# Head norms of a differential attention two at a time, and five waits moved, in an encoder trunk on one core

## The reference

```python
s = einsum('bhcqd,bhckd->bhcqk', q_blk, kt) * scale + bias      # two maps (c) for each of 4 heads
p = softmax(s, axis=-1)
a = p[:, :, 0] - lam * p[:, :, 1]
o = einsum('bhqk,bhkv->bhqv', a, vt)                            # 128 channels a head
o = rms_norm(o, subln_g) * (1.0 - lam_init)                     # per head, over its 128 channels
mixed = concatenate([u, o.reshape(B, T, DIFF_WIDTH)], axis=-1)  # u: the convolution module, 512 channels
h = h + mixed @ w_out
```

## Time and profile before

| | |
|---|---|
| time, median of 3 runs | 1874.54 us (1874.12 to 1876.93) |
| profiled execution | 1874.37 us |
| its span, first to last instruction | 1872.6 us |
| mean granted TensorE clock | 0.995 |
| PE busy | 1821.2 us (97%) |
| DVE busy | 1310.9 us (70%) |
| ACT busy | 829.0 us (44%) |
| POOL busy | 160.0 us (9%) |

### The profile page before, as it was taken

The page is one execution under the profiler, slowest core; times in us unless marked ns, Lnnn a source line. Parts: engine busy times, 40 slices in busy tenths (PEclk is TensorE's granted clock), DMA queues, the critical chain, the costliest instruction groups (busy, mean ns, idle before and its releaser), DMA issues.

```text
span 1872.6 us, 38843 instructions
## 1 busy us (share of the span) xinstructions
PE 1821.2 (97%) x16913; PEld 1495.9 (80%) x16913; DVE 1310.9 (70%) x1716; ACT 829.0 (44%) x1085; POOL 160.0 (9%) x127
## 2 busy tenths in 40 slices
PE   6999999999999999999999999999999999999998
PEld 4898657778888888885779999898778788888886
DVE  5898665435878687857748888887574347787867
ACT  4434675335544434423644334343553346343445
POOL 1000002001000000110002222222110010000001
PEclk9999999999999999999999999999999999999999
DMA  6226323203152331453432122112442113405231
GB/s 219 69 90 212 109 80 134 90 23 103 55 179 63 118 123 57 144 174 124 162 141 72 51 52 56 52 32 71 150 159 90 46 45 113 153 27 180 65 116 57
DMA packets 149842, 189.95 MB, mean 101 GB/s; under 512 B 11881, under 2 KB 119958, under 8 KB 148010
## 3 DMA queue, kind: packets, MB, share of 16 engines
q1 hardware_dynamic: 146352, 174.97, 29.3%
q0 software_dynamic: 3088, 12.45, 1.7%
q10 hardware_dynamic: 234, 0.06, 0.0%
HBM read 161.75 MB, written 21.51 MB: 98 GB/s over the span
## 4 chain that ended last, share of the span: by engine, by line
PE 52%; DVE 3%; ACT 1%; issue 1%; DMA 1%; DVEq 0%; ACTq 0%; SPq 0%
PE ps L408 10%; PE ps L410 10%; PE ps L409 10%; PE ps L2645 7%; PE ps L2611 2%; PE ps L2658 2%; PE ps L2599 1%; PE ps L1979 1%; PE ps L2019 1%; PE ps L2622 1%; PE ps L1397 1%; PE ps L2741 1%; PE ps L2578 1%; PE ps L2670 1%; PE ps L1378 1%
## 5 line engine op out<-in xcount | busy, mean ns | idle before, releaser
L372 DVE TENSOR_TENSOR weights_split<-w,weights_split 128x2048 fp32r<-128x2048 f32 x117 | 267.9, 2290 | 116.4 <-ACT weights_split L354 102.9
L354 ACT ACTIVATE weights_split<-w 128x2048 fp32r<-128x2048 f32 x118 | 226.3, 1918 | 266.8 <-PE ps L410 249.1
L408 PE MATMUL ps<-x_hn_hi,weights_split 128*128 128x512 f32 x640 | 252.4, 394 | 0.0
L410 PE MATMUL ps<-x_hn_hi,weights_split 128*128 128x512 f32 x640 | 249.2, 389 | 0.0
L409 PE MATMUL ps<-x_hn_lo,weights_split 128*128 128x512 f32 x640 | 249.0, 389 | 0.0
L408 PE MATMUL ps<-weights_split,f_hidden_hi 128*128 128x512 f32 x448 | 175.5, 392 | 0.0
L410 PE MATMUL ps<-weights_split,f_hidden_lo 128*128 128x512 f32 x448 | 174.5, 389 | 0.0
L409 PE MATMUL ps<-weights_split,f_hidden_hi 128*128 128x512 f32 x448 | 174.5, 389 | 0.0
L408 PEld LDWEIGHTS ps<-x_hn_hi,weights_split 128*128 128x128 f32 x640 | 120.2, 188 | 25.6 <-issue 1.0
L409 PEld LDWEIGHTS ps<-x_hn_lo,weights_split 128*128 128x128 f32 x640 | 120.2, 188 | 25.6 <-issue 1.0
L410 PEld LDWEIGHTS ps<-x_hn_hi,weights_split 128*128 128x128 f32 x640 | 120.1, 188 | 25.2
(11 more groups left out here) (395 smaller groups left out, 3771.8 us busy)
## 6 DMA issues: line engine op xcount, KB each, us to landing
w<-in_ffn_w_up_dram SPq DMA_DIRECT2D x24, 1024.0 KB, 7.4
w<-in_ffn_w_down_dram SPq DMA_DIRECT2D x24, 1024.0 KB, 5.3
w<-in_xattn_w_kv_dram SPq DMA_DIRECT2D x15, 1024.0 KB, 5.5
w<-in_ab_w_in_dram SPq DMA_DIRECT2D x10, 1024.0 KB, 5.1
w<-in_xattn_w_q_dram SPq DMA_DIRECT2D x8, 1024.0 KB, 5.2
w<-in_xattn_w_o_dram SPq DMA_DIRECT2D x8, 1024.0 KB, 5.1
f_weights<-in_ffn_w_up_dram SPq DMA_DIRECT2D x8, 1024.0 KB, 6.7
f_weights<-in_ffn_w_down_dram SPq DMA_DIRECT2D x8, 1024.0 KB, 5.3
```

Of the source, the lines that this page charges most:

```text
L354: act.activation(hi, raw, ACT.Copy).then_inc(k.w_hi_ready, 1)
L372: eng.tensor_tensor(lo, raw, hi.bitcast(F32), ALU.subtract).then_inc(k.w_lo_ready, 1)
L408: pe.matmul(out, lhs[0], rhs[0], start=start, stop=False, skip_group_check=shared)
L410: return pe.matmul(out, lhs[1], rhs[0], start=False, stop=stop, skip_group_check=shared)
```

## The change

It has six parts.

- First stage: the remainder of weight unit 13 moves from before tap 118 to before tap 115.
- Attention stage: each of the head's three buffers becomes two; the second ones lie in `k.sums0`, which is not in use in this stage. Heads 0 and 1 are normed together: "n" of both in step 11, "m" of both in step 12, "M" of both in step 13 (before: steps 7, 8, 9 and 11, 12, 13). Heads 2 and 3 are normed together in the tail. On ACT the two Ln come first, then the two Exp.
- Unit 0 is rounded in three parts on ACT, behind the transposes of steps 7, 8 and 10 (executed in steps 9, 10 and 12), and its remainder is taken in three parts on DVE behind the differences of steps 12, 13 and 14. The remainder of unit 1 follows the difference of step 15 (before: head 2's multiplies).
- The tail: the chunks of the projection are reordered; outputs 2 and 3 take chunk 4 before outputs 0 and 1 take chunks 6 and 7.
- RWKV: PE waits for the value input chunk by chunk in the first value tile.
- Second output projection: DVE takes unit 2's remainder before it waits for h.

The first two parts of the diff are new helpers; `round_third` and `rest_third` do columns 0 to 2, 3 to 5 and 6 to 7 of eight blocks of 256.

```diff
+    THIRDS = (slice(0, 3), slice(3, 6), slice(6, 8))
+    def round_third(self, act, i, g):
+        k, n, c = self.k, self.base + i, self.THIRDS[g]
+        raw, hi, _ = self.parts(n)
+        if g == 0:
+            k.w_wait(act, k.units[n][0])
+            act.wait_ge(*k.split_end[n - 2])
+        ins = act.activation(hi[:, c, :], raw[:, c, :], ACT.Copy)
+        if g == 2:
+            ins.then_inc(k.w_hi_ready, 1)
+            k.rounded += 1
+    def rest_third(self, dve, i, g):
+        ...
+        if g == 0:
+            dve.wait_ge(k.w_hi_ready, n + 1)
+            dve.wait_ge(k.w_lo_ready, n)
+        ins = dve.tensor_tensor(lo[:, c, :], raw[:, c, :], hi[:, c, :].bitcast(F32), ALU.subtract)
...
-        splits = {13: 4, 26: 5, 39: 6, 52: 7, 65: 8, 78: 9, 98: 10, 104: 11, 110: 12, 118: 13, 121: 14}
+        splits = {13: 4, 26: 5, 39: 6, 52: 7, 65: 8, 78: 9, 98: 10, 104: 11, 110: 12, 115: 13, 121: 14}
...
-        self.o = k.place(106 * KB, "head_out", [P, T])
-        self.osq = k.place(108 * KB, "head_sq", [P, T])
-        self.rs = k.place(110 * KB, "diff_rs", [P, T])
+        spare = [k.sums0[:, n, :] for n in range(3)]
+        self.o = [k.place(106 * KB, "head_out", [P, T])[:, :], spare[0]]
+        self.osq = [k.place(108 * KB, "head_sq", [P, T])[:, :], spare[1]]
+        self.rs = [k.place(110 * KB, "diff_rs", [P, T])[:, :], spare[2]]
...
-            for lag, kind in ((3, "o"), (4, "n"), (5, "m"), (6, "M")):
-                if i >= lag and (i - lag) % 4 == 3:
-                    order.append((kind, (i - lag) // 4, 0))
+            if i in (6, 10, 14):
+                order.append(("o", (i - 6) // 4, 0))
+            elif i in (11, 12, 13):
+                order += [("nmM"[i - 11], h, 0) for h in range(2)]
...
-        order += [("d", 15, 0), ("R", "01", "01"), ("m", 2, 0), ("t", 14, 0), ("R", "01", "23"), ("M", 2, 0),
-                  ("t", 15, 0), ("R", "23", "0"), ("o", 3, 0), ("R", "23", "1"), ("n", 3, 0), ("R", "01", "456"),
-                  ("R", "23", "23"), ("m", 3, 0), ("M", 3, 0), ("R", "01", "7"), ("R", "23", "4567")]
+        order += [("d", 15, 0), ("R", "01", "01"), ("t", 14, 0), ("R", "01", "23"), ("t", 15, 0), ("R", "23", "0"),
+                  ("o", 3, 0), ("R", "23", "1"), ("n", 2, 0), ("n", 3, 0), ("R", "01", "45"), ("R", "23", "23"),
+                  ("m", 2, 0), ("m", 3, 0), ("M", 2, 0), ("M", 3, 0), ("R", "23", "4"), ("R", "01", "67"),
+                  ("R", "23", "567")]
...
+                if i in (12, 13, 14):
+                    lay.ws.rest_third(dve, 0, i - 12)
+                elif i == 15:
+                    lay.ws.rest(dve, 1)
...
-                if h in (1, 2):
-                    lay.ws.rest(dve, h - 1)
...
+                if i in (7, 8, 10):
+                    lay.ws.round_third(act, 0, (7, 8, 10).index(i))
...
-                k.wait_freed(act, n)
-                act.activation(self.rs[:, :], self.rs[:, :], ACT.Exp, scale=-0.5).then_inc(self.s_rs, 1)
-                if i == 1:
-                    lay.ws.round(act, 0)
+                if i % 2:
+                    for h in (i - 1, i):
+                        k.wait_freed(act, num[("n", h, 0)])
+                        act.activation(self.rs[h % 2], self.rs[h % 2], ACT.Exp, scale=-0.5).then_inc(self.s_rs, 1)
...
-                    if c == 0:
-                        pe.wait_ge(pairs[g % 2].s_lo, 8 * (g // 2) + 8)
-                    mm = mm3_chunks(pe, k, n, ws, i, (c % 2) * P, pairs[g % 2].both)
+                    if x == ("v", 0):
+                        k.take(pe, n)
+                        for b in range(8):
+                            pe.wait_ge(pairs[0].s_lo, 8 + b + 1)
+                            mm = mm3(pe, k.bank(n), ws.pair(i, b, slice(0, P)), [y[:, b, :] for y in pairs[0].both],
+                                     b == 0, b == 7)
+                    else:
+                        mm = mm3_chunks(pe, k, n, ws, i, (c % 2) * P, pairs[g % 2].both)
...
         k.rested += 2
+        lay.ws.rest(dve, 2)
         dve.wait_ge(self.s_in2, 80)
```

More of the change, by code:

```diff
@@ L372, in subtract @@
         eng.tensor_tensor(lo, raw, hi.bitcast(F32), ALU.subtract).then_inc(k.w_lo_ready, 1)
+    THIRDS = (slice(0, 3), slice(3, 6), slice(6, 8))
+    def round_third(self, act, i, g):
+        k, n, c = self.k, self.base + i, self.THIRDS[g]
+        assert n == k.rounded
+        raw, hi, _ = self.parts(n)
[7 more added lines that the diff above has]
+        else:
+            k.act(ins)
+    def rest_third(self, dve, i, g):
+        k, n, c = self.k, self.base + i, self.THIRDS[g]
+        assert n == k.rested
+        raw, hi, lo = self.parts(n)
+        if g == 0:
+            dve.wait_ge(k.w_hi_ready, n + 1)
+            dve.wait_ge(k.w_lo_ready, n)
+        ins = dve.tensor_tensor(lo[:, c, :], raw[:, c, :], hi[:, c, :].bitcast(F32), ALU.subtract)
+        if g == 2:
+            ins.then_inc(k.w_lo_ready, 1)
+            k.rested += 1
+        else:
+            k.dve(ins)
     def wait(self, pe, i):
@@ L1049, in pe @@
                 k.wait_freed(pe, num[("o", i, 0)])
-                pe.matmul(k.bank(n), k.ones, self.osq[:, :], start=True, stop=True).then_inc(k.done(n), 1)
+                pe.matmul(k.bank(n), k.ones, self.osq[i % 2], start=True, stop=True).then_inc(k.done(n), 1)
             elif kind == "R":
@@ L1090, in dve @@
                 dve.wait_ge(self.s_oc, h + 1)
-                k.dve.link(dve, dve.tensor_tensor(o[:, :], o[:, :], self.rs[:, :], ALU.mult))
-                dve.tensor_scalar(self.cat[:, CC + h, :], o[:, :], k.p("diff_subln_g", 0), 1.0 - LAM_INIT,
+                o = self.o[h % 2]
+                k.dve.link(dve, dve.tensor_tensor(o, o, self.rs[h % 2], ALU.mult))
+                dve.tensor_scalar(self.cat[:, CC + h, :], o, k.p("diff_subln_g", 0), 1.0 - LAM_INIT,
                                   ALU.mult, ALU.mult).then_inc(self.s_om, 1)
-                if h in (1, 2):
-                    lay.ws.rest(dve, h - 1)
             elif kind == "M":
@@ L1133, in act @@
                 k.wait_full(act, n)
-                if h:
-                    act.wait_ge(self.s_om, h)
-                act.activation(self.o[:, :], k.bank(n), ACT.Copy).then_inc(self.s_oc, 1)
-                if h:
-                    k.wait_full(act, num[("n", h - 1, 0)])
-                act.activation(self.osq[:, :], k.bank(n), ACT.Square).then_inc(k.free(n), 1)
+                if h > 1:
+                    act.wait_ge(self.s_om, h - 1)
+                act.activation(self.o[h % 2], k.bank(n), ACT.Copy).then_inc(self.s_oc, 1)
+                if h > 1:
+                    k.wait_full(act, num[("n", h - 2, 0)])
+                act.activation(self.osq[h % 2], k.bank(n), ACT.Square).then_inc(k.free(n), 1)
                 if h == 2:
@@ L1143, in act @@
                 k.wait_full(act, n)
-                if i:
-                    act.wait_ge(self.s_om, i)
-                act.activation(self.rs[:, :], k.bank(n), ACT.Ln, bias=k.eps[:, 0:1], scale=1.0 / P) \
+                if i > 1:
+                    act.wait_ge(self.s_om, i - 1)
+                act.activation(self.rs[i % 2], k.bank(n), ACT.Ln, bias=k.eps[:, 0:1], scale=1.0 / P) \
                     .then_inc(k.free(n), 1)
-                k.wait_freed(act, n)
-                act.activation(self.rs[:, :], self.rs[:, :], ACT.Exp, scale=-0.5).then_inc(self.s_rs, 1)
-                if i == 1:
-                    lay.ws.round(act, 0)
+                if i % 2:
+                    for h in (i - 1, i):
+                        k.wait_freed(act, num[("n", h, 0)])
+                        act.activation(self.rs[h % 2], self.rs[h % 2], ACT.Exp, scale=-0.5).then_inc(self.s_rs, 1)
             elif kind == "m":
```

3 lines of the change are left out of this document (2 added, 1 removed).

## The result

| | before | after |
|---|---|---|
| median | 1874.85 us (1873.72 to 1876.93, 6 runs) | 1865.58 us (1863.57 to 1867.31, 6 runs) |
| profiled execution, its span | 1874.37, 1872.6 | 1865.52, 1863.7 |
| PE busy | 1821.2 | 1817.8 (98%) |
| ACT, instructions | 829.0, 1085 | 824.2, 1083 |

The ratio is 0.9949 [0.9937, 0.9962], so the changed kernel is 7 to 12 us faster (9.3 by the medians); the forecast was 1866.2.

The account below looks back on a forecast made before the run. The prediction took TensorE (PE), busy 97% of the span, as the bound, so time is won only where PE waits. It summed 1.6 + 4.45 + 1.6 + 0.6 = 8.3 us, 1874.5 to 1866.2, range 1863.4 to 1870.3.

Parts of the forecast that it names:

- Part 1: First stage: weight unit 13's remainder three taps earlier on DVE ends PE's wait for it, 1.6 us gained.
- Part 2: Attention stage: old stalls of 7.86 us go, new ones of 2.95 and 0.46 come, net 4.45 gained.
- the rest is a stretch at clock 0.50: Attention steps 7 to 10: of 4.02 us lost, two waits are 1.85, the remainder is PE at 1.2 GHz.
- half clock: Rival, attention stage: one new stall brings back PE's 1.2 GHz clock, costing 2.2 us, 1868.4; chance 0.13.
- not after the longer single one: Attention stage: PE's clock fell after two close waits, but stayed 1.00 after the long wait at 257.07.
- The walk: Attention stage's new stalls, followed step by step with row durations: 2.95 us in sum, leaving PE 4.91 ahead.
- Part 3: RWKV values: waiting chunk by chunk removes PE's wait for the last of eight remainders, 1.6 us gained.
- Part 4: Second output projection: unit 2's remainder ahead of the wait for h's reload, 0.6 us gained.
- Harder stalls: Rival, attention stage: the two-head block on ACT doubles the new stalls, saving only 5.3 us, 1869.2; chance 0.13.
- A longer switch: Rival, two-head block: each ACT table switch adds 1.29 us, step 13's bank 2.6 later, 1868.8; chance 0.02.
- Stalls only moved: Rival, attention stage: stalls only change places; parts 1, 3 and 4 remain, 3.8 us, 1870.7; chance 0.11.
- The first third's weights: Rival, attention step 9: unit 0's first third, at about 236.1, waits for its load; slower, 1878 at 20 us; chance 0.03.

Follow-up runs that it names:

- the four executions: Profiled executions of the attention stage's old order: the kernel before, unchanged, three times (1874.37, then 1874.89 and 1874.03 us), and the kernel before with parts 1, 3 and 4 (1871.01).
- the run: Changed kernel with unit 1's rounding on ACT moved from behind head 2's square to behind step 13's transposes (run in step 15): 1866.70 us, ratio 0.9948 to before.
- the kernel with all three moved: Changed kernel with unit 1's rounding and unit 0's last rounding third later, all three thirds of unit 0's remainder behind step 13's difference: 1863.89 us, ratio 0.9939 to before.
- the second: The kernel before, unchanged, profiled a second time: 1874.89 us in one run, span 1873.1.
- the third: The kernel before, unchanged, in a third profiled execution: 1874.03 us in one run, span 1872.2.
- four loads: Changed kernel with each head's Exp directly behind its Ln, so four table loads in place of two per pair of norms: 1869.91 us, ratio 0.9976 to before.
- the kernel with the rounding moved: Kernel before with units 0 and 1's rounding thirds and remainders in the changed kernel's places, norms one at a time as before: 1871.93 us against 1876.10, ratio 0.9978.
- the kernel with the three waits alone: Kernel before with only parts 1, 3 and 4 of the change, the attention stage as before: 1871.01 us, ratio 0.9984.
- remainder alone moved: Changed kernel with the last third of unit 0's remainder on DVE moved from behind step 14's difference to behind step 13's: 1867.48 us in one run.
- both moved: Changed kernel with unit 1's rounding behind step 15's transposes' copy and the last third of unit 0's remainder behind step 13's difference: 1864.39 us, ratio 0.9938 to before.

## Why the prediction was right, and where it wasn't

**Part 1** (1.6 forecast). Measured 1.55, and 1.56 or 1.57 in the eight other kernels that hold it. The changed kernel's DVE and PE there:

```profile
156.43 2.30 DVE L372 TENSOR_TENSOR weights_split<-w,weights_split 128x2048 fp32r<-128x2048 f32 x1
158.63 4.08 DVE L946 SCALAR_TENSOR_TENSOR cat<-glu,par,cat 128x512 f32<-128x512 f32 x6
162.61 2.31 DVE L372 TENSOR_TENSOR weights_split<-w,weights_split 128x2048 fp32r<-128x2048 f32 x1
```

```profile
157.00:164.00 7.00, 7.00 (x61) 7.00 (x60) 7.00 (x8) 2.58 (x3) 0.00 (x0) 1.00 0.59 192
```

Unit 13's remainder ends at 158.7, the six taps follow it, and PE has no idle time in the window. Unit 14's, which the prediction saw fit by under 0.1, fits: no PE row behind it has idle time.

**Part 2** (4.45). The total, 4.50, is right against the profile it was made from. Its terms: the block on ACT was forecast at 4.95 and took 4.93. The new stalls, read from start to start, are 0.59 in step 12, 0.12 in step 13 (forecast 0.07 and 0.66: right in sum, one row earlier), 0.96 in step 14 (0.88), 1.35 before the projection (1.34) and 0.47 at unit 2 (0.46). The moved pieces that were costed at nothing show in no row of PE.

Two readings in it were wrong, and neither shows in the sum (its "steps 8 and 9" for the two waits is a slip: by its own rows both lie in step 9):

- "the rest is a stretch at clock 0.50". The 4.02 lost in steps 7 to 10 is real, but 2.2 of it isn't a price of the clock: with the clock at 1.00 the long wait's row stands at the same place. PE is late there because ACT is. The rival "half clock" was therefore priced from the wrong stretch; what such a fall costs where no other engine is late behind it is 1.6 to 1.7, the stretch behind the long wait.
- "not after the longer single one". Two of the four executions have it there. The first profile happened to show the cheaper case, so the forecast took the price of before too low by what the others lose: (0 - 0.03 + 1.66 + 1.55) / 4 = 0.8 on average. That this equals the 0.8 by which the medians lie further apart than the four parts is in part chance: part 4's stretch is longer than the first profile's in every other execution of the old code (below), part 3 gains less in most, and the interval of the medians' difference is 5 us wide. So the forecast was right term by term for the pair of profiles, and its nearness to the medians, 8.3 against 9.3, is also luck.

The walk named ACT's key copy as what holds the projection, and said nothing of the last third of the remainder on DVE, which ends 0.19 before it. For the forecast it was of no consequence; whoever had gone on to improve the kernel by that walk would have gained 0.1 instead of 1.1, as the run did.

**Part 3** (1.6). 1.65 in this profile, 1.64 in the kernel with all three moved, 1.2 to 1.4 in the seven others that hold it. The seven added waits show no idle time on PE in any of them, and why the seven gain less stays open. The size is right to 0.4.

**Part 4** (0.6). 0.78 against the first profile. The wait that it removes isn't of one size: DVE stood before the reload of h, and PE's row shows 0.49 idle in the first profile, 1.08 in the second and 1.25 in the third, and 0.68 and 0.79 in the two other kernels that leave this part as it was. DVE of the third, and of the changed kernel, which no longer waits for the transfer:

```profile
1385.50 2.29 DVE L372 TENSOR_TENSOR weights_split<-w,weights_split 128x2048 fp32r<-128x2048 f32 x1 [6.95 <-DMA h_again<-d_h]
```

```profile
1376.16 2.29 DVE L372 TENSOR_TENSOR weights_split<-w,weights_split 128x2048 fp32r<-128x2048 f32 x1 [4.68 <-ACT weights_split L354]
```

By stretches the changed kernel gains 0.78, 1.35 and 1.55 against the three executions of before, 0.95 and 1.04 against the other two. Here, too, one profile showed the lower end.

**The rivals.** Half clock: in the eight executions of the new stage with two loads a pair the clock is 1.00 in every 5 us of it; their longest wait is 1.28. With 0.90 and 1.77 close together (four loads) it fell, in the one execution profiled. Harder stalls: 3.49 in sum where 3.41 was forecast. A longer switch: the block's 4.93 leaves no room. Stalls only moved: of 7.86, 3.02 came back in new places and 0.47 at unit 2, where 2.95 and 0.46 were forecast. The first third's weights: it ran at 233.20, 38.15 after the stage's first product (forecast 236.1 in the times of before, 37.95), and waited for no transfer.

The Trainium skill, "ScalarE: Activation LUTs", section "What ACT_TABLE_LOAD costs", puts a switch at a load of 1.28 and a drain that bring it to 2.66. The four-load block takes 7.78 for four loads (5.1) and four activations (2.6): this chip's trace shows no drain between them.

## What to carry to other kernels

Where several engines meet at one instruction, list the end of every semaphore it waits for, not only the one that the profile names: two pieces of work that ended 0.2 us apart had to be moved together, and either alone brought 0.1 or nothing. Price a stall by what is late behind it, not by its row: a slowed stretch of PE behind which another engine was late anyway cost 0.1 here, and a like stretch elsewhere 1.6. Before a forecast of a few us, look at a second execution of the same kernel, since waits on a transfer and falls of the clock differ between them.

## What was not expected of the hardware

**Whether the clock falls after a given stall differs by execution.** After the same idle time of 2.19 us it fell in two of four executions of the old order. After the two waits of 0.39 and 0.80 it fell in four of five: those four and the kernel with the rounding moved, the exception being the kernel with the three waits alone. An earlier fall doesn't decide the later one: of the three old executions with the first fall one had the second too, and the one without the first had it. The order of the work and its waits are the same, so something besides them decides. The Trainium skill, "TensorE: Matmul & The Clock Gate", section "Part 1: The HAM clock gate", describes a monitor that runs free of the kernel, so that the same kernel meets it at another phase each time; the rows fit that and don't prove it.

**The first stage differs by 1.5 us between executions, and the granted clock goes with it.** From PE's row at 23.02 to the one at 142.65 (times of the first profile of before) it took 118.2 in the seven executions whose clock was 1.00 from 35 us on, and 119.6 to 120.1 in the six whose clock fell between 40 and 50 us. One, the kernel with all three moved, took 119.8 with a fall at 29 to 33 us. Windows of the first profile of before, of the second, and of the changed kernel:

```profile
45.00:50.00 5.00, 4.89 (x15) 3.96 (x16) 0.06 (x1) 0.00 (x0) 0.51 (x1) 0.68 0.16 50
```

```profile
45.00:50.00 5.00, 5.00 (x24) 4.12 (x23) 0.00 (x0) 0.00 (x0) 0.02 (x1) 1.00 0.05 12
```

```profile
45.00:50.00 5.00, 5.00 (x22) 4.16 (x23) 0.00 (x0) 0.00 (x0) 0.41 (x1) 1.00 0.14 46
```

So the 1.55 in the first line of the table of stretches isn't the change's: the second and the third execution of before reach the same row 1.92 and 1.37 earlier than the first. The scan (379.3 us, from 976.81 to 1356.12 in the first profile) took between 1.8 less and 4.8 more in the other executions, though no kernel changes it. The two longest, 382.3 (remainder alone moved) and 384.1 (both moved), are the only ones in which the clock fell in the scan, to 0.50 for 3 us or so, the second time behind a wait of 2.23 us for which the profile names no releaser; the other differences are waits of tenths to 1 us at a few recurring rows. What decides them stays open. That is why single runs were read by stretches here.
